# Reordering the first head pair, the last pair's gate steps and the expert whose weights come ahead

## The reference, cut to what matters

```python
# block 1
mod = silu(c) @ w_ada + b_ada                       # shift, scale, gate (3 x 1024)
h = rms_norm(x, g) * (1 + scale) + shift
proj = h @ w_in
r, k, v, g, wd, ad = split(token_shift(proj[..., :2176], mu))
w_log = -softplus(-(w0 + tanh(wd) @ w2)) - 0.5      # low-rank step 1: decays
a = sigmoid(a0 + ad @ a2)                           # low-rank step 2
kk = normalised(k * k_k);  k = k * (1 + (a - 1) * k_a)
y_r = scan(rwkv7_step, (r, exp(-exp(w_log)), k, v, -kk, kk * a))   # 8 heads of 64
x = x + gate * (concat(y_r * silu(g), band_attention(...) * silu(g_a)) @ w_out)
# block 2
x = x + g_m * hybrid_mixer(...)                     # modulation from silu(c_2) @ ada_w_2
for each of 32 experts (2 chosen per token, through a router of 4 groups x 8):
    y += weight * (silu(x_e @ w_gate[e]) * (x_e @ w_up[e])) @ w_down[e]
out = rms_norm(x + g_f * y) * final_g
```

## Time and profile before

| | us |
|---|---|
| median of 3 runs | 1387.43 |
| lowest, highest | 1385.04, 1387.83 |
| the profiled execution: its time | 1388.69 |
| its span in the trace | 1387.0 |

### The profile page before, as it was taken

One profiled execution on the slowest core, in us unless ns is written; L12 is line 12 of the kernel. 1 busy time (PEld: TensorE's weight loads), 2 busy tenths in 40 slices (PEclk: granted clock), 3 DMA queues, 4 the chain that ended last, 5 costly groups with the idle time before them and its releaser, 6 DMA issues.

```text
span 1387.0 us, 20749 instructions
## 1 busy us (share of the span) xinstructions
PE 1280.7 (92%) x7392; PEld 638.6 (46%) x7393; DVE 612.6 (44%) x1058; ACT 351.2 (25%) x759; POOL 160.1 (12%) x278
## 2 busy tenths in 40 slices
PE   4989999998999999999999999999999987898886
PEld 1446666566854444554445555433333322333222
DVE  1477787874213343349686625312222212122115
ACT  1322332421135442221467510101111101111012
POOL 4011111102020000000000001411122211121110
PEclk9999999999999999999999999999999999899999
DMA  9172534330173110014212384789999999999995
GB/s 372 63 259 72 185 121 168 138 108 17 48 234 102 46 46 0 0 66 152 61 53 115 138 341 191 270 340 400 396 374 418 401 406 422 408 405 408 413 397 215
DMA packets 40570, 304.00 MB, mean 219 GB/s; under 512 B 7980, under 2 KB 8132, under 8 KB 22944
## 3 DMA queue, kind: packets, MB, share of 16 engines
q1 hardware_dynamic: 31952, 285.12, 52.4%
q0 software_dynamic: 8528, 17.67, 4.0%
HBM read 299.49 MB, written 13.75 MB: 226 GB/s over the span
## 4 chain that ended last, share of the span: by engine, by line
PE 67%; DMA 16%; DVE 9%; ACT 3%; issue 3%; POOL 2%; DVEq 0%; SPq 0%; ACTq 0%; POOLq 0%
PE bank L885 19%; DMA arena<-in_w_down 13%; PE bank L2986 10%; PE bank L816 8%; PE bank L3004 7%; PE bank L931 3%; PE bank L993 2%; PE bank L2971 1%; PE bank L1007 1%; DMA arena<-in_ada_w 1%; PE bank L1232 1%; PE bank L1176 1%; DVE side L1518 1%; PE bank L1153 1%; PE bank L920 1%
## 5 line engine op out<-in xcount | busy, mean ns | idle before, releaser
L885 PE MATMUL bank<-hT,arena 128*128 128x512 f32 x656 | 290.8, 598 | 0.0
L2986 PE MATMUL bank<-arena,hT 128*64 128x512 f32 x1012 | 230.8, 606 | 16.9 <-DMA arena<-in_w_gu 16.9
L885 PEld LDWEIGHTS bank<-hT,arena 128*128 128x128 f32 x656 | 123.3, 191 | 147.4 <-issue 144.1
L2986 PEld LDWEIGHTS bank<-arena,hT 128*64 128x64 f32 x1012 | 72.0, 139 | 155.6 <-issue 134.1
L3004 PE MATMUL bank<-arena,yT 128*64 128x512 f32 x512 | 124.3, 630 | 14.0 <-DMA arena<-in_w_down 12.2
L3174 DVE TENSOR_SCALAR hT<-hT 128x256 f32<-128x256 f32 x32 | 9.4, 295 | 249.0 <-ACT hT L3112 249.0
L816 PE MATMUL bank<-arena,yT 128*128 128x512 f32 x256 | 116.1, 608 | 2.4 <-DVE yT L1778 2.3
L3112 ACT ACTIVATE hT<-bank 128x256 f32<-128x256 f32 x32 | 12.3, 384 | 264.8 <-PE bank L2986 264.8
L816 PEld LDWEIGHTS bank<-arena,yT 128*128 128x128 f32 x256 | 48.6, 194 | 61.1 <-issue 57.3
L931 PEld LDWEIGHTS bank<-arena 64*64 64x64 f32 x1856 | 60.1, 136 | 26.1 <-issue 12.2
L3004 PEld LDWEIGHTS bank<-arena,yT 128*64 128x64 f32 x512 | 36.2, 143 | 77.3 <-issue 61.4
(11 more groups left out here) (498 smaller groups left out, 1672.1 us busy)
## 6 DMA issues: line engine op xcount, KB each, us to landing
arena<-in_w_gu SPq DMA_DIRECT2D x62, 2048.0 KB, 27.0
arena<-in_w_down SPq DMA_DIRECT2D x32, 2048.0 KB, 30.3
arena<-in_w_in SPq DMA_DIRECT2D x53, 512.0 KB, 3.6
arena<-in_ada_w SPq DMA_DIRECT2D x24, 1024.0 KB, 5.4
arena<-in_w_ada SPq DMA_DIRECT2D x8, 1024.0 KB, 9.5
arena<-in_w_out SPq DMA_DIRECT2D x8, 1024.0 KB, 9.0
arena<-in_w_ada SPq DMA_DIRECT2D x8, 512.0 KB, 7.2
arena<-expert_rows SPq DMA_DIRECT2D x4, 1024.0 KB, 8.8
```

What stands on the lines that cost most here:

```text
L885: last = T.matmul(bank[0:rows, :], w[:, k, 0:rows], hT[:, k, :], start=k == 0, stop=k == KD - 1)
L2986: last = T.matmul(banks[1 + ub][MT * h:MT * h + MT, :], tile.xT[:, k, :], weights[:, :, 256 * h:256 * h + 256], start=k == 0, stop=k == KD ...
```

## The change

In the first pair `lora(0)` goes ahead of the receptance projection on TensorE, and ScalarE and VectorE take the decays ahead of the receptance's copy and shift. VectorE makes the operands ahead of the shift of the value, so TensorE waits for that shift before it turns the operands (`s_shift`). Of the eight modulation steps three stay where they were, and five go behind the grams; `dve_ada(1)` goes behind the first masked factor Tc and ahead of the masked grams. In the last pair the gate steps go from 2, 2, 2, 2 at levels 1 to 4 to 0, 2, 3, 3. The expert whose part is loaded ahead becomes number 28 (the 29th), and with it round 9 becomes straight code and round 2 joins the loop.

```diff
--- before.py
+++ after.py
@@ -171,6 +171,7 @@
             plan(("proj", p, j), "act")
 
         PROJ_ORDER = (1, 0, 2, 3)
+        ADA_EARLY = 3
 
         def plan_lora(p):
             plan(("zw", p), "act")
@@ -183,8 +184,8 @@
             plan(("hT", 0, k), "act" if k % 2 else "dve")
         plan(("wa",), "act")
         plan_proj(0, 1)
+        plan_lora(0)
         plan_proj(0, 0)
-        plan_lora(0)
         plan(("kk", 0), "dve")
         plan_proj(0, 2)
         plan(("bonus", 0), "dve")
@@ -968,14 +969,14 @@
             pe_norm(0, range(EARLY, KD))
             pe_proj(("wa",), wait_hT=True)
             pe_proj(("proj", 0, 1))
-            pe_proj(("proj", 0, 0))
             eng.wait_ge(s_small, 32)
             eng.wait_ge(s_tw, 1)
             lora(0)
+            pe_proj(("proj", 0, 0))
             key_norm(0)
             pe_proj(("proj", 0, 2))
             eng.wait_ge(s_first_in, 1)
-            for k in range(KD):
+            for k in range(ADA_EARLY):
                 pe_ada(1, k)
             bonus(0)
             for p in range(PAIRS):
@@ -1018,6 +1019,8 @@
                     full(last)
 
                 eng.wait_ge(s_ops, 3 * p + 1)
+                if not p:
+                    eng.wait_ge(s_shift, ITEM[0, 2] + 1)
                 for c in range(TT):
                     bank = fill(("tok", p, c))
                     for i, src in enumerate((alr[p % 2][:, c, 0, :], t_b[:, CH(c)], t_k2[:, CH(c)], sh[:, 2, CH(c)])):
@@ -1026,6 +1029,9 @@
                 gram_low(p)
                 gram_up(p, 1, 0, t_b)
                 gram_up(p, 2, 1, t_b)
+                if not p:
+                    for k in range(ADA_EARLY, KD):
+                        pe_ada(1, k)
                 if p:
                     mean(p - 1)
                     mod_rows(1 + p)
@@ -1042,8 +1048,8 @@
                     elif q:
                         gate_steps(1)
                     else:
-                        if l <= 4:
-                            gate_steps(2)
+                        if 1 < l <= 4:
+                            gate_steps(2 if l == 2 else 3)
                         va_rows(2 if l <= 4 else 1)
                     wait_emptied(eng, ("W", p, l))
                     if l > 1:
@@ -1272,10 +1278,10 @@
                                              bias=modc[0][:, k:k + 1]), ("hT", 0, k))
             bank = take(S, ("wa",))
             empty(S, "act", S.activation(raw[:, 0, 1:513], bank[:, :], ACT.Copy), ("wa",))
-            proj_raw(0, 0)
             eng.wait_ge(s_first_in, 2)
             act.done(S.activation(TW[0:64, :], TW[0:64, :], ACT.Exp, scale=2.0))
             eng.sem_inc(s_tw_exp, 1)
+            proj_raw(0, 0)
 
             def lora_exp(p):
                 bank = take(S, ("zw", p))
@@ -1323,13 +1329,13 @@
                 act.done(S.activation(t_g, gsh[:, p % 2, :], ACT.Exp, scale=-1.0))
                 eng.sem_inc(s_yg, 1)
 
+            lora_exp(0)
+            key_square(0)
+            decay_sigmoid(0)
             proj_raw(0, 1)
-            key_square(0)
-            lora_exp(0)
-            decay_sigmoid(0)
+            decay_exp(0)
             key_norm(0)
             proj_raw(0, 2)
-            decay_exp(0)
             for p in range(PAIRS):
                 q = p + 1 if p + 1 < PAIRS else None
                 for c in range(TT):
@@ -1629,14 +1635,13 @@
             eng.sem_inc(s_tw, 1)
             eng.wait_ge(s_const, C_BLOCK1)
             proj_shift(0, 0)
+            decay_clamp(0)
+            decays(0)
+            key_norm_in(0)
             proj_shift(0, 1)
-            decay_clamp(0)
-            key_norm_in(0)
-            decays(0)
             bonus_in(0)
+            operands(0)
             proj_shift(0, 2)
-            operands(0)
-            dve_ada(1)
             bonus_out(0)
             eye8 = ident_half.rearrange("p (o t) -> p o t", o=1).to_broadcast([P, 8, HD])
             tri2 = tri.rearrange("p (o a) t -> p o (a t)", o=1).to_broadcast([P, 2, 2 * P])
@@ -1676,6 +1681,8 @@
                 dve.done(V.tensor_tensor(Tc, LTc, level_up[:, 0:1, 0:HD].to_broadcast([P, 8, HD]), MUL))
                 dve.done(V.tensor_tensor(Tc, Tc, eye8, ADD))
                 eng.sem_inc(s_ops, 1)
+                if not p:
+                    dve_ada(1)
                 gram_masked(p, 1, LbT, 0)
                 gram_masked(p, 2, LbT, 1)
                 if p:
@@ -2694,7 +2701,7 @@
         slot_w = [arena[:, 12288 * at:12288 * (at + 1)] for at in (2, 1, 0)]
         FIRST = (1, 2, 0)
         first_slot = FIRST.index
-        AHEAD, AHEAD_STEPS = 2 * U + 2, 3
+        AHEAD, AHEAD_STEPS = (ROUNDS - 1) * U + 1, 3
         wgu = [w[:, 0:8192].rearrange("p (h k a n) -> p h k a n", h=2, a=2, k=KD // 2) for w in slot_w]
         wdn = [w[:, 8192:12288].rearrange("p (a n) -> p a n", a=4) for w in slot_w]
         yflat = yT[:, :, :].rearrange("p k t -> p (k t)")
@@ -2753,16 +2760,17 @@
         def experts(eng, body):
 
 
-            for it in (1, 2):
+            for u in range(U):
+                body(1, u, U + u)
+            later_experts(eng, body)
+
+        def later_experts(eng, body):
+
+            with eng.Fori(2, ROUNDS - 1) as it:
                 for u in range(U):
                     body(it, u, it * U + u)
-            later_experts(eng, body)
-
-        def later_experts(eng, body):
-
-            with eng.Fori(3, ROUNDS) as it:
-                for u in range(U):
-                    body(it, u, it * U + u)
+            for u in range(U):
+                body(ROUNDS - 1, u, (ROUNDS - 1) * U + u)
             for u in range(REST):
                 body(ROUNDS, u, ROUNDS * U + u)
```

## The result

| | before | after |
|---|---|---|
| median of 4 runs, us | 1387.41 | 1372.84 |
| lowest, highest | 1385.04, 1387.83 | 1371.18, 1375.67 |
| the profiled execution: its time, its span | 1388.69, 1387.0 | 1375.67, 1374.0 |

The ratio is 0.9903, 95% interval 0.9887 to 0.9919: 13.5 us faster (11.2 to 15.7), where 14.8 was forecast; the two medians lie 14.6 us apart. The profiled execution of after is the slowest of its four, and the two traces differ by 13.0.

The account below looks back on a forecast made before the run. TensorE was taken to bind to about 1100 us, the stream of weights behind it. Gains of 5.4 + 6.9 + 2.5 = 14.8 us gave a median of 1372.6 us, forecast 1370.3 to 1374.5, wider range 1369.5 to 1379.5.

Parts of the forecast that it names:

- (a): First pair: low-rank products move ahead of the receptance projection, TW ready about 53.6 us, TensorE waiting 0.6 us.
- (b): First pair: early exponentials put the operands at 71.0 us and the value's shift at 72.5, before the transposes at 73.15.
- (d): First pair, five late modulation steps: the eighth waits 1.4 us for its weights; W blocks start 4.4 us earlier (2.9 to 4.9).
- (e): First pair: the shorter wait wins back 1.0 of 1.5 us lost at half clock (bounds 0 and 1.5).
- (f): First pair: VectorE 1.8 us late for D of level 1, hidden by 4 us of other TensorE work.
- Part 2: Last pair: moving the gate steps gains 6.9 us, 5.17 of waiting and 1.77 of half clock (bounds 5.2 and 6.9).
- D 12 us earlier: Sign in the last pair: D was to come 12 us earlier than before, from 5.4 + 6.9.
- Part 3: Experts' stage: loading ahead for expert 28 instead of 8 fills the stream's idle gap, 2.5 us (bounds 0 and 3.8).
- The growing wait: Rival, first pair: late step's weights queue with chunks, VectorE late too; gain 1 instead of 5.4 us, 1377.0; chance 0.13.
- The tail gives nothing: Rival, experts' stage: TensorE's own chain or a slower stream sets the end; 1375.1 us; chance 0.18.
- cost of straight code: Rival, experts' stage: late code stalls five bodies behind the loop, 20.8 us; slower by 8.5, 1395.9; chance 0.03.

## Why the prediction was right

**(a), (b) low-rank steps and operands: right.** All counted from the start of the first projection (38.24 before, 37.41 after): products forecast at 15.4, seen at 15.2; TensorE's wait for TW forecast at 0.6, seen 0.8; `operands` ended at 70.4 and the value's shift at 72.0, so transposes started at 34.8 (34.9 forecast) without a wait. It was closer than forecast: the shift ended 0.16 us ahead of them, where 0.6 of slack was worked out. With late steps alone TensorE waits 4.2 us for the operands, with early operands alone its own steps hold it: both chains have to move.

**(d) the last step's wait: right.** 1.30 us against 1.4, and the run with four steps ahead shows that the send behind the fourth step caused it. From send to use it took 3.8 us (77.69 to 81.52), with four chunks sent right behind it, 0.2 more than the 3.6 of the load sent into an empty queue; 4.1 was taken. The trace doesn't agree with the 3.2 us estimated from the Trainium skill ("DMA: Bandwidth & Descriptors", Anatomy of one DMA), whose section fits loads that GpSimd sends, while this one goes by the sync engine.

**(e) the clock: mis-sized.** All of the 1.5 us came back, 1.0 was taken. It did so in all five traces with late steps and early operands. The 1.5 is itself a property of the trace read: behind the same wait of 2.93 us the eight traces that have it lose 1.4 to 3.1 us.

**(f) VectorE behind `dve_ada`: the cover failed in part.** VectorE was late by 3.4 us instead of 1.8 (counted from the first projection, its second load landed 1.3 us later than forecast, and D came 0.4 us sooner, mostly since the W blocks did), and I let DT, grams and low-rank steps hide it. They do for D itself, but za, the second low-rank product, goes to the bank that D of level 1 leaves, and the planner hands out banks in turn: seven fills after D comes za. TensorE waited 0.48 us there, and the two products, side by side in 0.96 us elsewhere, went one after the other in 2.55. From D of level 1 to W of level 2 the after trace takes 6.40 us against 4.80. So of 6.2 us gained at D in the two profiled executions 4.6 were left at level 2, where 5.4 were forecast: 0.3 more at the W blocks and 0.5 more from the clock against 1.6 lost here. The errors don't cancel. Over all traces (four with the edit, seven without) it is 6.7 at D and 4.9 at level 2, since the other kernels start the W blocks 0.8 us later on average than the trace that was read. That the times show 5.3 is in part luck.

**Part 2: right in mechanism, a little small.** 7.5 us against 6.9. The wait and the half clock went; D came 0.2 us sooner than worked out, two steps moved to later levels cost 1.7 us, not 1.9, and the traces without the edit lost 0.2 us more on average than the one I had read. One sign was worked out wrongly: "D 12 us earlier" took the two gate steps off already, which at D are still to come. By the prediction's own numbers it is 5.4 + 8.8 = 14.2 us, and 14.8 were seen.

**Part 3: right in sign and mechanism, size open.** The dry time was filled. 2.9 us (0.8 to 5.0) in the times against 2.5, but 1.6 in the traces, where the stage scatters by 5 us. A cost stands against it that the prediction didn't see: with the stream full TensorE waits once more, 2.4 to 4.4 us for a gather (the last section has the rows). How much of the gain that wait takes no run shows. In the profiled execution of after the last down weights came only 12.5 us earlier, not 14 to 15: its experts' stage took 473.1 us against 472.1. In the same kernel run again it took 469.6.

**Rivals.** The growing wait is out as priced; its second half, VectorE late, cost 1.6 of its 4.4 us. "The tail gives nothing" is out by the experts' part alone, narrowly (0.8 us at the least). No cost of straight code was seen: the waits without a releaser stand at the same two points of the stage whichever rounds are straight. On the clock the skill warns of a long DMA wait between every matmul (Trainium skill, "TensorE: Matmul & The Clock Gate", Loop structure matters more than you think). For the single wait of 1.3 us in the first pair the trace doesn't show such a loss; behind some of the repeated waits for weights in the experts' stage, of 1.2 to 1.7 us, it does (rows in the last section).

The version to keep is the whole change with four steps ahead, by its traces: median 1370.04 us, though the times alone don't tell it from three.

## What to carry to other kernels

Where two chains meet, move both or neither: here each alone was worth nothing. When work is moved behind a point, look at what its last instruction releases: the send of the next buffer moved with it, and moving one step back ahead of the grams mended two waits. And for a late engine, ask who wants its bank next in the planner's turn, not only who wants its result.

Bytes saved from a stream count only where the stream binds, and before the last thing that is waited for: ahead of expert 8 they turned into idle time in five traces of seven, and at the last expert they came behind the weights that set the end.

## What the hardware showed beyond that

- The length of a wait alone doesn't say what the clock does behind it. In the first and the last pair TensorE's work took no longer than elsewhere behind waits of 1.30 and 1.40 us (1.15 and 1.96 us for W blocks and two gate steps). Behind 2.93 us the W blocks took 1.98 us at a granted clock of 0.50 in the kernel before, and the 2 us after 90 ran at 0.67. In the run of the gate steps alone they still took 1.15 at 1.00 behind the same wait, and the projection after them fell to 0.51 and took 8.83 instead of 7.13. Behind 4.18 and 5.17 us the clock was 0.59 and 0.50 (3.21 for 1.91, 3.75 for 1.98 us).
- In the experts' stage, where one short wait follows another, a wait of 1.16, 1.43 or 1.66 us for down weights was followed by a product of 5.3 us at a granted clock of 0.68, others of 1.10 and 1.75 us by one of 3.65 us at 1.00. Two of them in the kernel before:

```profile
1277.73 3.65 PE L3004 MATMUL bank<-arena,yT 128*64 128x512 f32 x16 [1.75 <-DMA arena<-in_w_down]
1309.91 5.31 PE L3004 MATMUL bank<-arena,yT 128*64 128x512 f32 x16 [1.43 <-DMA arena<-in_w_down]
```

- TensorE stands 3.6 to 4.2 us, in every trace of this study, before the transposes of an expert 330 to 336 us into the experts' stage, with no releaser named; in nine of the fourteen it also does so, for 2.4 to 4.4 us, at 152 to 158 us. These nine are exactly the traces without the dry time, whatever was loaded ahead. GpSimd's timeline points to the reason, first before, then after, with TensorE's wait after below them:

```profile
1012.53 0.18 POOL L2892 CAST place_col<-iotas 128x1 uint32<-128x1 f32 x1 [2.18 <-DMA expert_rows<-cactB,place_col]
1005.06 0.18 POOL L2900 CAST place_col<-iotas 128x1 uint32 x1 [6.72 <-DMA expert_rows<-cactB,place_col]
1008.48 0.98 POOL L2895 DMA_INDIRECT yT<-xn_scratch,idx_col  x1 [1.02 <-issue]
1018.44 1.12 PE L2979 MATMUL bank<-ident,yT 64*128 64x64 f32 x8 [3.81 <-issue]
```

  GpSimd waits for its scatter of the rows of an expert with more than 64 tokens to land before it sends the next gather. That wait is 2.2 to 3.0 us in the five traces with the dry time and 4.8 to 7.3 in the nine others; ahead of the later wait of TensorE it is 7.1 to 7.5 in all fourteen. The gather then leaves late, and TensorE starts some 10 us behind it. No experiment moved the scatter, so the cause is read from traces, not tested.
- The experts' stage varied by up to 5 us between traces of kernels that do the same work there, more than anything the third part could give.
